# Fewer convolution taps left to the feed-forward stage: 12 and 12 in place of 36 and 28

## What is computed

```python
h = rmsnorm(x, g_mix)
a, gate, q, k, v = split(h @ w_in)            # 512, 512, 8x64, 8x64, 8x64 columns
u = a * sigmoid(gate)
c = causal_depthwise_conv(concat(past_conv, u), w_dw) + b_dw      # 31 taps, 512 channels
c = silu(layernorm(c, g_cn, b_cn)) @ w_pw
q, k = rmsnorm per head
o = stick_breaking_attention(q, concat(past_k, k), concat(past_v, v))   # strictly causal, 8 heads
x = x + concat(c, o) @ w_out
x = x + relu(rmsnorm(x, g_ff) @ w_ff1)**2 @ w_ff2
return x, k, v, last 30 rows of concat(past_conv, u)
```

## Time and profile before

| | |
|---|---|
| median of 3 runs | 2974.12 us (2970.78 to 2979.04) |
| the profiled execution | 2970.43 us, span 2968.6 us |
| mean granted TensorE clock | 0.971 of full speed |
| PE busy | 2754.2 us, 93% |
| DVE busy | 1638.2 us, 55% |
| ACT, POOL busy | 1084.7 us, 758.1 us |

### The profile page before, as it was taken

The page is one execution under the profiler, slowest core; times in us unless marked ns, Lnnn a source line. Parts: engine busy times, 40 slices in busy tenths (PEclk is TensorE's granted clock), DMA queues, the critical chain, the costliest instruction groups (busy, mean ns, idle before and its releaser), DMA issues. The chain is left out here.

```text
span 2968.6 us, 37403 instructions
## 1 busy us (share of the span) xinstructions
PE 2754.2 (93%) x13936; PEld 2290.0 (77%) x13936; DVE 1638.2 (55%) x2457; ACT 1084.7 (37%) x2177; POOL 758.1 (26%) x622
## 2 busy tenths in 40 slices
PE   7678878999999999999999998899999999999999
PEld 6556666677878787778888796677888877898887
DVE  5886785746664366547665257644777742212122
ACT  4323533345654113235554212243666631121111
POOL 4532444335554022013222002201333310000000
PEclk9899889899999999999999999999999999999999
DMA  8586587766666758555554744743554447353442
GB/s 298 204 280 229 171 286 255 278 237 238 245 245 251 280 193 278 212 193 179 185 196 176 305 171 166 253 181 135 179 180 158 160 151 272 118 208 128 185 156 89
DMA packets 262047, 616.19 MB, mean 208 GB/s; under 512 B 23217, under 2 KB 159409, under 8 KB 213741
## 3 DMA queue, kind: packets, MB, share of 16 engines
q1 hardware_dynamic: 261869, 613.80, 57.8%
HBM read 444.79 MB, written 168.94 MB: 207 GB/s over the span
## 5 line engine op out<-in xcount | busy, mean ns | idle before, releaser
L1143 POOL TENSOR_TENSOR beta<-beta,stay 128x512 f32<-128x512 f32 (+3 forms) x328 | 325.2, 994 | 728.4 <-DVE stay L1798 728.3
L1936 PE MATMUL ps<-h2T_hi,w_s 128*128 128x512 f32 (+1 forms) x1280 | 467.9, 366 | 7.3 <-DMA w_s<-w_scratch 3.2
L1937 PE MATMUL ps<-h2T_lo,w_s 128*128 128x512 f32 (+1 forms) x1280 | 455.7, 356 | 0.0
L1938 PE MATMUL ps<-h2T_hi,w_s 128*128 128x512 f32 (+1 forms) x1280 | 455.5, 356 | 0.0
L2190 PE MATMUL ps<-w_s,hid_hi 128*128 128x512 f32 (+1 forms) x1088 | 435.2, 400 | 12.0 <-DVE hid_lo L1869 12.0
L2191 PE MATMUL ps<-w_s,hid_lo 128*128 128x512 f32 (+1 forms) x1088 | 426.2, 392 | 0.0
L2192 PE MATMUL ps<-w_s,hid_hi 128*128 128x512 f32 (+1 forms) x1088 | 425.8, 391 | 0.0
L1869 DVE TENSOR_TENSOR hid_lo<-ps,hid_hi 128x512 fp32r<-128x512 f32 (+1 forms) x160 | 95.6, 597 | 472.4 <-ACT hid_hi L1502 472.4
L1420 ACT ACTIVATE stay<-ps 128x512 f32<-128x512 f32 (+3 forms) x328 | 173.4, 529 | 427.2 <-DVE ps L1786 216.1
L1864 DVE TENSOR_TENSOR resid<-ps,resid 128x512 f32<-128x512 f32 x256 | 174.3, 687 | 244.1 <-PE ps L2192 243.6
L1057 POOL TENSOR_TENSOR w_s<-w_raw,w_s 128x1024 fp32r<-128x1024 f32 x94 | 243.5, 2612 | 243.8 <-ACT w_s L1200 243.8
(11 more groups left out here) (196 smaller groups left out, 4975.5 us busy)
## 6 DMA issues: line engine op xcount, KB each, us to landing
w_s<-w_scratch SPq DMA_DIRECT2D x282, 1024.0 KB, 7.7
w_scratch<-w_s SPq DMA_DIRECT2D x94, 1024.0 KB, 7.9
w_raw<-in_w_ff SPq DMA_DIRECT2D x64, 512.0 KB, 5.1
a_k<-k_scratch SPq DMA_DIRECT2D x80, 256.0 KB, 3.8
a_v<-v_scratch SPq DMA_DIRECT2D x80, 256.0 KB, 4.0
a_q<-q_scratch SPq DMA_DIRECT2D x64, 256.0 KB, 4.4
w_raw<-in_w_in SPq DMA_DIRECT2D x20, 512.0 KB, 7.9
mix_scratch<-ohl SPq DMA_DIRECT2D x66, 128.0 KB, 2.6
```

The source lines that it names most:

```text
L1143: nc.gpsimd.tensor_tensor(v[0:q.r, 0:n], v[0:q.r, 0:n], stay[q.z % 3][0:q.r, 1:n + 1], ALU.mult).then_inc(s_a, 1)
L1936: nc.tensor.matmul(out, w[0], x[0], start=start, stop=False)
L1937: nc.tensor.matmul(out, w[0], x[1], start=False, stop=False)
L1938: return nc.tensor.matmul(out, w[1], x[0], start=False, stop=stop)
```

## The change

One line: the number of taps that chunks 2 and 3 leave to the window.

```diff
-LATE = [20, 43, 36, 28]
+LATE = [20, 43, 12, 12]
```

## The result

The changed kernel takes 2985.98 us (median of nine runs, 2981.17 to 2990.33), the kernel before beside it 2975.79 us (nine runs, 2970.78 to 2980.96): ratio 1.0034, interval 1.0024 to 1.0045, or 10.2 us more. The forecast was 7.5 us more.

A forecast was written before the change was run, and what follows sets the result against it. TensorE, busy for 93% of the span, was taken as the bound. Chunk 2's +10.0 and chunk 3's -2.5 us gave +7.5 on 2974.1, so 2981.6 us; the forecast's own range 2975 to 2988, eight in ten 2968 to 2995.

The forecast's parts named there:

- The taps, 6.4 and 2.7 us: Taps added beside the projections exceed DVE's waits, so PE is late: 6.4 us in chunk 2, 2.7 in chunk 3.
- my rival of the projections as DVE's stage: POOL operations stretch beside longer tap runs, 1.8 us a query event, 12.6 us in all, some 2994; chance 0.25, slower.
- My own sign of being wrong: In the projections: the prediction is wrong if POOL's operations stretch beside the longer runs of taps.
- The store wait, 6.2 and 1.7 us of clock: Chunk 2, slot 8: PE's variance waits 6.2 us for squares held by query stores, plus 1.7 us of lost clock.
- the 5 to 7 that I gave as a sign: Both windows: ACT's squares wait 5 to 7 us for `q_scratch`, as does PE at the variance in slot 8.
- the forecast of 4.5 us for 6.2: Chunk 3, slot 8: a 4.5 us variance wait replaces the 6.2 us wait for `hid_lo`, a gain of 1.7.
- The slab, -4.9 + 0.6: Chunk 2, earlier pointwise projection: 3.2 us slab wait and 1.7 us of clock gained, 0.6 lost on its own slabs.
- Chunk 3's projection and attention, -1.85 and -1.65: Chunk 3: projection waits fall from 6.2 to 4.35 us, gaining 1.85; wider-spread attention gains 1.65 at the turn.
- Scaling a wait by the share of double slots: Chunk 3 attention: 15.9 us turn wait times 8/77, for 8 fewer slots with two steps, gives 1.65 us.
- The sum: Chunk 2 +10.0 and chunk 3 -2.5, together +7.5 us.
- the rivals with a hidden cost: Lateness, store wait or both hidden: one hidden some 2973 us, chance 0.20; both hidden some 2964.6, chance 0.10.

The follow-up runs named there:

- small gain product: Changed kernel, but POOL multiplies only one head of eight by the gain in chunks 2 and 3: 2978.14 us, ratio 0.9996 to the kernel before.
- taps and norm only: Changed kernel, but pointwise projection and attention stay in their old slots: 2997.37 us, ratio 1.0067 to the kernel before.
- taps only: Changed kernel, but norm, pointwise projection and attention keep their old slots, only the taps move: 2987.74 us, ratio 1.0037 to the kernel before.
- wait later: Changed kernel, ACT's wait for the query stores moved from the norm's squares to its gate step, convolution state out six slots later: 2963.11 us, ratio 0.9958 to before.
- three taps a slot: Kernel before with ACT's store wait moved later, window taps of chunks 2 and 3 three to a slot: 2966.03 us, ratio 0.9965 to before.

## Why the prediction was right, and which step was wrong

**The taps, 6.4 and 2.7 us.** Measured as the growth of `kvq`: 5.8 and 4.0. Size and place hold: in chunk 2 DVE has no idle time from the third value event on (in chunk 3 it still stood 1.8 and 4.0 us in two query events), and PE's turns wait 4.8 and 3.2 us more for ACT's copies. The reason, the taps' time less DVE's waits, fits as well, since DVE's busy time grew by 0.64 us for each added instruction. (Key events got 7 taps more, not the 8 of the text, which changes nothing in the sum.) But what I did not see is that DVE's time there already held meetings with POOL's product. I had read only the one POOL row of 2.81 us as such a meeting and overlooked that `packed` took 1.38 us in chunk 2's query events, twice what the like subtraction of `vpack` took the earlier trace rows. After the change `packed` takes 0.69 us there, and the taps bear the delay, about 1.0 us an event. That was the mechanism of my rival of the projections as DVE's stage, but the cost that the rival added to the sum, 1.8 us an event, is not there. My own sign of being wrong, POOL's operations that stretch beside the longer runs, came too (the product at 1150.24 took 2.83 us for 1.30), without the term being wrong for it: in chunk 2's query events DVE never stood for POOL's result. What the meetings cost is 3.2 us of `kvq(2)` after the change (the small gain product); how much of that the kernel before paid stays open, so of the 5.8 us at least 2.6 are the taps' own. A share of the lateness is order as well: scaling after four taps takes 3.3 us off with the product in place.

**The store wait, 6.2 and 1.7 us of clock.** 7.0 us of waiting (the recorded numbers make 6.3: 1198.0 less 1191.7); the wait moved away is worth 9.4 us in slots 0 to 7. The step was right and 1.5 us small: the half clock lasted 6.8 us, in which PE was busy for 4.2 us and so lost 2.1. The landing time taken from the earlier trace rows, 7.8 us, is the median of the four stores after. ACT itself stood for 13.4 us, not the 5 to 7 that I gave as a sign; PE felt the end of that. In chunk 3 the forecast of 4.5 us for 6.2 came out as 4.7, and taps and norm only against taps only gives a gain of 2.0 for the 1.7.

**The slab, -4.9 + 0.6.** The wait is gone and 0.6 remains, as said. Two runs size the gain. With the wait later chunk 2 takes 692.0, that is 691.7 + 3.9 for the taps (from the run with taps only) - 3.6; but the run with taps only happens to lack the stretch at half clock behind the slab wait, 1.7 us of PE's time, and with it the taps cost 5.6 and the gain is 5.3. Holding the projection back costs 7.0, with a stretch at half clock in which PE was busy for 6.1 us and lost 3.0, in place of 1.7, so 5.7 against before. Chunk 3 of the run with three taps a slot has the same wait at the same slot 30.

**Chunk 3's projection and attention, -1.85 and -1.65.** The projection's waits came as worked out: 4.1 us in three (forecast 4.35) and none for a slab. The attention's did not: 15.4 for 15.9, 0.5 us in place of 1.65, and a wider spread made them longer in another kernel. Scaling a wait by the share of double slots has no support left. The run that held both back costs 5.2 us all the same; PE idles for 2.3 of it and is busy for 2.9, of which 1.7 is a stretch of 3.4 us at half clock. The waits that the trace names differ by 0.8 us or less each, and the cause of the rest is open.

**The sum.** +10.0 and -2.5 were forecast, +10.0 and -1.0 measured. That chunk 2 came out to the tenth is luck: the store wait with its clock was 1.5 us more than its 7.9, the slab's gain about 1 us more than its 4.3, and the taps about 0.6 less. In chunk 3, too, errors cancel: held back step by step, the taps cost 6.2 us (taps only), the norm gave 2.0 and projection with attention 5.2, against 2.7, 1.7 and 3.5 in the sum. So every term had the right sign, and the largest miss is chunk 3's taps, 3.5 us. Of that, 1.3 is the longer `kvq(3)` and the rest is not followed. Of the rivals with a hidden cost, none came: each cost is seen by itself.

## What to carry to other kernels

Before work is moved out of a stage with slack, look at the waits of the work that will follow it forward: here the norm ran into stores that land 8 us after their issue. Placing the wait where the buffer is written gave 15.4 us with no tap moved, and packing the taps more densely where they were gave chunk 2 its 7 us without the lateness; in chunk 3 the denser taps were 9.7 us slower. A stage in which an engine is 70% busy has no room where its events are already back to back; read the room event by event. And look for the same instruction at two durations: 1.38 and 0.69 us in the trace of before were the sign of a collision that was there already. To tell whether a change adds to it, compare the engine's busy time for the same work, not one instruction.

## What the runs showed of the hardware

**DVE and POOL hold one another up.** In some events the taps wait: a run that POOL's product meets is 1.0 us longer (5.10 for 4.05 us) and the product takes 1.68. In others the product waits: one that started inside a run ended 1.2 us after the run's end, 4.81 us for 1.30. What decides between the two is not shown. Kernels with the same taps in chunk 3 took 106.5 to 110.6 us for `kvq(3)`: 1.6 of that is clock, as said above, and in the two longest DVE was busy for 75.2 us in place of 74.1. The Trainium skill (SBUF — State Buffer, the section on SBUF's two separate sides) says that such a pair is locked for the whole of the earlier instruction. These rows agree, and better than I judged beforehand; that a product stands through the rest of a run of several DVE instructions, 3.5 us here, goes beyond its single instruction.

**The same wait, three stretches of clock.** Behind the slab wait of 3.2 us before, the granted clock was 0.50 (1.2 GHz) for 3.4 us. The run with taps only has the same wait (3.1 us) and a clock of 1.00 (2.4 GHz) throughout the 35 us around it; the run that held the projection back (3.3 us) has 0.50 for 6.8 us. Windows of the first two, columns as above:

```profile
1288.30:1291.70 3.40, 3.40 (x10) 2.65 (x9) 0.00 (x0) 0.00 (x0) 0.00 (x0) 0.50 1.01 426
```
```profile
1285.00:1320.00 35.00, 31.39 (x146) 25.40 (x145) 10.36 (x19) 13.25 (x28) 4.35 (x5) 1.00 0.75 303
```

A price for clock behind a short wait is, by these runs, uncertain by its own size.
